# Second attention's projections in packed weight tiles

## The chip, the cores and the metric

The kernel runs on one core of one Trainium2 chip. The time is the device time of one execution in microseconds (us); the time before is a median of three runs. The profile shows one execution. Its engines are PE (TensorE, the matrix engine, with PEld for its weight loads), DVE (VectorE), ACT (ScalarE), POOL (GpSimd) and SP (SyncE, which issues the DMAs).

## The reference, cut to what matters

The program computes two transformer blocks on 512 tokens of width 1024. The second has a sparse attention (8 heads, called NSA here) and a second, latent attention (8 heads, MLA). Only the latter's projections change:

```python
def mla_attention(c_q, c_kv, k_rope, positions, q_norm_g, w_q_up, kv_norm_g, w_kv_up):
    q = (rms_norm_2(c_q, q_norm_g) @ w_q_up).reshape(B, S, H, MLA_NOPE_DIM + MLA_ROPE_DIM)
    q_nope = q[..., :MLA_NOPE_DIM]
    q_rot = rope(q[..., MLA_NOPE_DIM:], positions)
    kv = (rms_norm_2(c_kv, kv_norm_g) @ w_kv_up).reshape(B, S, H, MLA_NOPE_DIM + MLA_V_DIM)
    k_nope, v = kv[..., :MLA_NOPE_DIM], kv[..., MLA_NOPE_DIM:]
    k_rot = rope(k_rope[:, :, None, :], positions)[:, :, 0]
    scale = (MLA_NOPE_DIM + MLA_ROPE_DIM) ** -0.5
...
        s = (jnp.einsum('bqhd,bkhd->bhqk', qn, k_nope)
             + jnp.einsum('bqhd,bkd->bhqk', qr, k_rot)).astype(jnp.float32) * scale
        p = masked_softmax(s, key_idx[None, :] <= tc[:, None])
        return jnp.einsum('bhqk,bkhd->bqhd', p.astype(v.dtype), v)
```

A head's query has 64 plain and 32 rotated values; its key has 64 plain values of its own and the 32 rotated ones that all heads share. `w_q_up` is 256 x 768, `w_kv_up` 128 x 1024.

## The kernel before, in words

Each engine runs a program written out by hand. It waits on semaphores that count the steps of the others: `after(engine, who, name)` waits until `who` has done the step `name`, `done` marks a step, and the lists `STEPS` hold each engine's steps in order. Nothing is reordered while it runs.

The attention is a loop over 96 steps on every engine: steps 0 to 63 are NSA (query tiles of 128 by head and branch), 64 to 95 are MLA (eight heads `e` with four query tiles `qt` each, which see 128, 256, 384 and 512 keys). In step i TensorE runs

- `scores(i)`, queries as weights against the keys as moving data (L2854; the lines here are those of the profile);
- `fill(i, 4)`: four matmuls of the other work's stream, the input projections z0 to z7 up to step 63, nothing in steps 64 to 69, and the output projections oA, oB, oC from step 70 (`A_FIRST`), L2114;
- `jobs(i)`, odd work that belongs to certain steps;
- `turned(i - 2)` (L2863), two more matmuls of the stream, and `values(i - 3)` (L2877).

DVE takes the maximum of the scores (`most`) and adds the values up (`combine`), ACT does the exponential (`soft`) and copies the turned probabilities; each then has its own `jobs(i)`.

MLA's projections are such jobs. Head h has three: `q up h` in step 58 + 4h (two matmuls with 96 weight columns, L2689, one for each half of 256), `k up h` in the next step (one with 64 columns, L2695) and `rot up h` in the next (one with 96 rows and columns, which swaps the halves of the rotated part, L2701). ACT copies q up to `qraw` and k up to `km`; POOL multiplies `qraw` by the cosines (`rcos`, L1335), DVE the turned values by the sines (`rsin`, L2042) and adds the two to `qm` (L2047, step `q ready h`). The 64 plain rows pass through both with cosine 1 and sine 0. `qm` and `km` hold two heads. DVE copies the shared rotated keys to both halves of `km` once (L2034). `latent values c` (L2680, steps 63 to 66) makes the value rows of a token chunk.

The jobs write to two banks in turn: `aux_bank` gives a job one of them by its place in the table `JOBS`, and `job_free` waits for the reader of the job two places before.

At the change from NSA to MLA a chain begins. When the 64 NSA steps are added up, TensorE turns o_nsa (steps 67 and 68, L2706), DVE multiplies it by the gate (`mix`, step `mixed k`, L1925) into one of two buffers, ACT rounds it to `hhi` (`mix high k`, L1098), POOL takes the rest as `hlo` (`mix low k`, L1316) and frees the buffer. oA0 in step 70 waits for `mixed 3`, which frees its banks, and at each k for `mix low k`. A weight tile of the stream comes by SP's queue into one of four slots of `stage`, ACT rounds it to `whi` (L1001), POOL takes the rest as `wlo` (L1264).

Of the kernel before, what the change touches and what calls it, by code (L numbers as in the profile page):

```python
# [75 lines left out]
for _step in range(58, N_STEPS):  # L76
    if 63 <= _step < 67:
        JOBS[f"latent values {_step - 63}"] = ("act", f"latent values {_step - 63}")
    if _step < 58 + 4 * QH and _step % 4 == 2:
        JOBS[f"q up {(_step - 58) // 4}"] = ("act", f"ev q up {(_step - 58) // 4}")  # L80
    if 59 <= _step < 59 + 4 * QH and _step % 4 == 3:
        JOBS[f"k up {(_step - 59) // 4}"] = ("act", f"ev k up {(_step - 59) // 4}")
    if 60 <= _step < 60 + 4 * QH and _step % 4 == 0:
        JOBS[f"rot up {(_step - 60) // 4}"] = ("dve", f"sin up {(_step - 60) // 4}")
    if _step in (75, 83, 91):
        JOBS[f"turned {4 + (75, 83, 91).index(_step)}"] = ("dve", f"mixed {4 + (75, 83, 91).index(_step)}")
# [35 lines left out]
def shape_constants_2():  # L122
# [34 lines left out]
def build(nc, A, out, const_cols, const2_cols):  # L157
# [3 lines left out]
    with ctx:  # L161
# [187 lines left out]
        for name in """ident_in const_in nm_in nm_tr nm_col ones_set ba_hi eps_set x_sq x_rms x_inv x_dg xtr xev rs_ps x_f h_hi h_lo vec_in vec_tr vec_col out_done w_hi w_lo w_used n_sq n_acc  # L349
# [2595 lines left out]
```

## Time and profile before

| | us |
|---|---|
| median of 3 runs (1146.34 to 1147.6) | 1146.76 |
| the profiled execution | 1146.54 |
| its span in the profile | 1144.7 |
| PE busy | 1112.0 (97%) |
| DVE, ACT, POOL busy | 585.6, 469.9, 488.0 |
| PE waiting for another engine, from 940 on, all together | 5.0 |

The difference between the profiled execution and its span, 1.8 us, lies around the span. The profile counts an fp32 matmul of 512 columns as two records, so an "x2" in a timeline row is one matmul, and for L2689 an "x4" is one projection. A row's duration is that from its first start to its modelled last end, and overlaps the next row; what something costs TensorE is read from start to start.

### The profile page before, as it was taken

To read this page: it belongs to the slowest core of one execution; us is meant where nothing else is said; L and a number is where in the kernel's file an instruction comes from. 1 tells how busy PE (TensorE), PEld (TensorE's weight loads), DVE (VectorE), ACT (ScalarE), POOL (GpSimd) and SP (SyncE) were. 2 spreads that over 40 slices of the span, in tenths; PEclk is the share of its full clock that TensorE was granted. 3 is DMA by queue.
4 is the path that set the end of the run, shared out by engine and by line. 5 is a ranking of instruction groups with operands and counts; after the bars stand their busy time and mean duration, and the time that the engine had idled before them with its cause. 6 is when DMAs were issued, how large, how long until landed. Compare 5 with 4: busy or idle time off the path is not lost. (4 is left out here: it accounts for less than half of the span.)

```text
span 1144.7 us, 16590 instructions
## 1 busy us (share of the span) xinstructions
PE 1112.0 (97%) x5905; PEld 908.2 (79%) x5905; DVE 585.6 (51%) x1250; ACT 469.9 (41%) x1004; POOL 488.0 (43%) x281
## 2 busy tenths in 40 slices
PE   7999999999999999999999999999999999999996
PEld 6788888888878878878888888867888888556674
DVE  6687656665646556512112126446653664344466
ACT  6544346555543431431331233433333444343343
POOL 5776412232326775764574574453121211132220
PEclk9999999999999999999999999999999999999998
DMA  7544522211105354354354355332112100001011
GB/s 217 141 113 125 138 56 66 56 55 48 38 19 171 96 165 147 93 166 139 99 165 128 111 158 129 95 74 56 38 38 65 47 20 28 12 9 38 19 38 74
DMA packets 161046, 99.84 MB, mean 87 GB/s; under 512 B 24056, under 2 KB 154444, under 8 KB 159948
## 3 DMA queue, kind: packets, MB, share of 16 engines
q1 hardware_dynamic: 160812, 98.80, 29.8%
q8 instruction: 45, 0.74, 0.3%
q14 instruction: 29, 0.24, 0.1%
q10 hardware_dynamic: 160, 0.07, 0.0%
HBM read 95.69 MB, written 3.16 MB: 86 GB/s over the span
## 5 line engine op out<-in xcount | busy, mean ns | idle before, releaser
L1172 POOL TENSOR_TENSOR wlo<-stage,whi 128x1024 fp32r<-128x1024 f32 (+1 forms) x105 | 273.0, 2604 | 238.5 <-ACT whi L712 238.3
L2114 PE MATMUL ps<-hhi,whi 128*128 128x512 f32 (+1 forms) x728 | 297.8, 409 | 3.9 <-DVE gated L1925 2.2
L2114 PE MATMUL ps<-hhi,wlo 128*128 128x512 f32 (+1 forms) x728 | 293.9, 404 | 0.0
L2114 PE MATMUL ps<-hlo,whi 128*128 128x512 f32 (+1 forms) x728 | 285.0, 395 | 0.0
L2114 PEld LDWEIGHTS ps<-hhi,whi 128*128 128x128 f32 (+1 forms) x728 | 137.0, 188 | 44.4 <-issue 13.5
L712 ACT ACTIVATE whi<-stage 128x1024 fp32r<-128x1024 f32 x104 | 109.6, 1055 | 129.1 <-PE ps L2114 100.2
L1264 POOL TENSOR_TENSOR wlo<-stage,whi 128x1024 fp32r<-128x1024 f32 (+3 forms) x40 | 73.5, 1838 | 197.8 <-ACT whi L1001 197.8
L2114 PEld LDWEIGHTS ps<-hlo,whi 128*128 128x128 f32 (+1 forms) x728 | 137.0, 188 | 24.0
L2114 PEld LDWEIGHTS ps<-hhi,wlo 128*128 128x128 f32 (+1 forms) x728 | 137.4, 189 | 22.8 <-issue 2.8
L1078 ACT ACTIVATE prob<-ps,aneg 128x128 f32<-128x128 f32 (+1 forms) x96 | 50.7, 528 | 199.5 <-issue 102.2
L2114 PE MATMUL ps<-ahi,whi 128*128 128x512 f32 x320 | 127.8, 399 | 4.7 <-POOL alo L1252 3.0
L2114 PE MATMUL ps<-alo,whi 128*128 128x512 f32 x320 | 125.2, 391 | 0.0
L2114 PE MATMUL ps<-ahi,wlo 128*128 128x512 f32 x320 | 125.1, 391 | 0.0
L1683 DVE TENSOR_TENSOR hf<-relu 128x512 f32<-128x512 f32 x32 | 26.8, 837 | 113.3 <-ACT relu L977 109.7
L1689 DVE TENSOR_TENSOR xT<-xT,ps 128x512 f32<-128x512 f32 x32 | 22.0, 688 | 103.0 <-PE ps L2114 103.0
L2114 PEld LDWEIGHTS ps<-ahi,whi 128*128 128x128 f32 x320 | 60.2, 188 | 18.1 <-POOL alo L1252 4.7
L2114 PEld LDWEIGHTS ps<-alo,whi 128*128 128x128 f32 x320 | 60.1, 188 | 12.3
L2114 PEld LDWEIGHTS ps<-ahi,wlo 128*128 128x128 f32 x320 | 60.2, 188 | 11.1
L1981 DVE SCALAR_TENSOR_TENSOR o_nsa<-ps,acoef,o_nsa 128x64 f32<-128x64 f32 x64 | 18.1, 283 | 85.2 <-PE ps L2877 84.9
L1388 DVE SCALAR_TENSOR_TENSOR acc<-ps,convw,acc 128x511 f32<-128x511 f32 (+2 forms) x72 | 53.8, 747 | 11.6 <-ACT acc L745 9.9
L1951 DVE TENSOR_REDUCE amax<-ps 128x1 f32<-128x128 f32 (+1 forms) x96 | 46.8, 487 | 25.0 <-PE ps L2855 24.1
L977 ACT ACTIVATE relu<-ps 128x512 f32<-128x512 f32 x32 | 19.1, 598 | 93.8 <-PE ps L2114 93.8
(378 smaller groups left out, 1834.7 us busy)
## 6 DMA issues: line engine op xcount, KB each, us to landing
stage<-dn_w_in SPq DMA_DIRECT2D x32, 512.0 KB, 4.1
stage<-mlp_w_up SPq DMA_DIRECT2D x32, 512.0 KB, 4.6
stage<-mlp_w_down SPq DMA_DIRECT2D x32, 512.0 KB, 4.6
mod_w<-ada_w SPq DMA_DIRECT2D x8, 1536.0 KB, 6.3
stage<-w_in SPq DMA_DIRECT2D x17, 512.0 KB, 3.6
gcrow<-gc_rows SPq DMA_DIRECT2D x16, 256.0 KB, 3.3
stage<-dn_w_out SPq DMA_DIRECT2D x8, 512.0 KB, 3.6
stage<-w_in SPq DMA_DIRECT2D x9, 256.0 KB, 2.9
```

The lines of the kernel that those rows point to most:

```text
L712: act.activation(whi[:, slot, 0:ks, 0:cols], stage[:, slot, 0:ks, 0:cols], ACT.Copy).then_inc(s["w_hi"], 1)
L977: act.activation(relu[:, m % 2], up_bank(q, m), ACT.Relu).then_inc(s["mlp_relu"], 1)
L1078: act.activation(prob[:, i % 2, 0:keys], ps[:, 2 + i % 2, 0:keys], ACT.Exp, scale=SCALE if kind == "nsa" else SCALE_M, bias=aneg[:, i % 2: ...
L1172: pool.tensor_tensor(wlo[:, slot, 0:ks, 0:cols], stage[:, slot, 0:ks, 0:cols], whi[:, slot, 0:ks, 0:cols], ALU.subtract).then_inc(s["w_lo" ...
L1264: pool.tensor_tensor(wlo[:, n % RING, 0:ks, 0:cols], stage[:, n % RING, 0:ks, 0:cols], whi[:, n % RING, 0:ks, 0:cols], ALU.subtract).then_ ...
L1388: dve.scalar_tensor_tensor(out=a[:, t:T], in0=u[:, 0:T - t], scalar=convw[:, (3 - t) * 3 + seq, h:h + 1], in1=a[:, t:T], op0=ALU.mult, op1 ...
L1683: dve.tensor_tensor(af[:, m % 2], relu[:, m % 2], relu[:, m % 2], ALU.mult).then_inc(s["mlp_f"], 1)
L1689: dve.tensor_tensor(xT[:, m], xT[:, m], ps[:, (U_MLP + m) % 2, :], ALU.add).then_inc(s["res"], 1)
L1951: dve.tensor_reduce(amax[:, c], ps[:, 2 + i % 2, 0:(qt + 1) * P], AX.X, ALU.max).then_inc(s["at_max"], 1)
L1981: dve.scalar_tensor_tensor(out=o, in0=ps[:, 7, 0:DK], scalar=acoef[:, c], in1=o, op0=ALU.mult, op1=ALU.add)\
L2114: mm = pe.matmul(bank, w[:, slot, k - ks[0], 0:width], x[:, k], start=(i == 0), stop=(i == len(todo) - 1))
```

## The change

The 96-column tile of a head is taken apart. `wqr` holds the rotated parts of four heads side by side (4 x 32 = 128 columns, `q rope g`, g = 0 or 1), `wqn` the plain parts (two heads, 128 columns, `q up j`), `wkn` the plain keys (two heads, 128 columns, `k up j`). `rot up g` turns four heads at once. The plain parts go from the bank straight to their place: ACT copies each result in two halves of 64 rows, and cosine, sine and sum are made only on the rotated parts.

The scores then run over 128 rows rather than 96. A head's query tile holds its 64 plain rows and 64 rows with the rotated parts of itself and of another head. The key tile `km` has four slots: 64 plain rows, 32 rotated key rows against the head's own part (`rope_rows`), and 32 zero rows against the other's. POOL clears `km` in step 46 (`key rows`), and SP copies the rotated keys in by four DMAs in place of DVE's copies. `qm` is now `q2T`, whose NSA queries have been used by then.

The core of the diff (the step lists are left out; the table `JOBS` and the step numbers stand for them):

```diff
+JOBS.update({"q rope 0": ("act", "ev q rope 0"), "rot up 0": ("dve", "sin up 0"),
+             "q up 0": ("act", "ev q up 0"), "k up 0": ("act", "ev k up 0")})
+JOBS.update({f"latent values {_c}": ("act", f"latent values {_c}") for _c in range(CH)})
...
+ROPE_STEP, PAIR_STEP = (54, 71), (60, 66, 76, 84)
...
+        def rope_rows(h):
+
+            first = (1 - h % 2) * MN + h % 4 // 2 * MR
+            return slice(first, first + MR)
...
                 if name == "z5":
                     after(sp, "dve", "post q3")
-                    sp.dma_start(wq[:, :, :, :], A["w_q_up_2"][0].rearrange("(k p) (h c) -> p k h c", p=P, c=MD)).then_inc(s["wq_in"], 16)
+                    w_q = A["w_q_up_2"][0].rearrange("(k p) (h c) -> k p h c", p=P, c=MD)
+                    for k in range(2):
+                        for g, odd in itertools.product(range(2), range(2)):
+                            sp.dma_start(wqr[:, k, g, 2 - 2 * odd:4 - 2 * odd], w_q[k, :, 4 * g + odd:4 * g + 4:2, MN:])                                .then_inc(s["wq_in"], 16)
+                    for k in range(2):
+                        sp.dma_start(wqn[:, k], w_q[k, :, :, 0:MN]).then_inc(s["wq_in"], 16)
...
+                if name == "z7":
+                    after(sp, "pool", "key rows")
+                    after(sp, "dve", "post kr")
+                    for h in range(4):
+                        sp.dma_start(km[rope_rows(h), h], krT[MN:MD, :]).then_inc(s["kr_in"], 16)
...
+                if i in ROPE_STEP:
+                    g = ROPE_STEP.index(i)
+                    after(act, "pe", f"q rope {g}")
+                    if g:
+                        after(act, "dve", "z 7")
+                    done(act.activation(qraw[g][:, :], aux_bank(f"q rope {g}"), ACT.Copy), f"ev q rope {g}")
+                for j in range(QH // 2):
+                    for what, dst in enumerate((qm, km)):
+                        if i == PAIR_STEP[j] + what:
+                            name = f"{'qk'[what]} up {j}"
+                            after(act, "pe", name)
...
+                            for r in range(2):
+                                ins = act.activation(dst[group(r), 2 * j % 4 + r], aux_bank(name)[group(r)], ACT.Copy)
+                            done(ins, f"ev {name}")
...
+                if i in (57, 58, 59, 65, 77, 78, 79, 82):
+                    h = (57, 58, 59, 65, 77, 78, 79, 82).index(i)
+                    after(dve, "dve", f"sin up {h // 4}")
+                    after(dve, "pool", f"cos up {h // 4}")
+                    dve.wait_ge(s["at_s"], 16 * (h + 1) if h < 4 else N_NSA + 4 * (h - 3))
+                    r = group(1 - h % 2)
+                    done(dve.tensor_tensor(qm[r, h % 4], rcos[r, :], rsin[r, :], ALU.add), f"q ready {h}")
...
                     if qt == 0:
                         after(pe, "dve", f"q ready {e}")
-                        after(pe, "act", f"ev k up {e}")
-                    q, k = qm[0:MD, e % 2, qt * P:(qt + 1) * P], km[0:MD, e % 2, 0:(qt + 1) * P]
+                        after(pe, "act", f"ev k up {e // 2}")
+                        pe.wait_ge(s["kr_in"], 64)
+                    q, k = qm[:, e % 4, qt * P:(qt + 1) * P], km[:, e % 4, 0:(qt + 1) * P]
```

How the order changes, at three places. TensorE, from the job of step 66 to that of step 68, before (wkv,cn is `latent values 3`, cn,wq `q up 2`, cn,wkv `k up 2`, qraw `rot up 2`):

```order
L2680 MATMUL ps<-wkv,cn 128x512
L2689 MATMUL ps<-cn,wq 96x512 x2
L2863 MATMUL ps<-const,prob 128x128
L2877 MATMUL ps<-v_1_116,probT 128x64 x4
L2854 MATMUL ps<-km,qm 128x512
L2855 MATMUL ps<-negb,identb 128x128
L2695 MATMUL ps<-cn,wkv 64x512
L2706 MATMUL ps<-const,o_nsa 128x128 x8
...
L2855 MATMUL ps<-negb,identb 128x128
L2701 MATMUL ps<-qraw,const_121 96x512
L2706 MATMUL ps<-const,o_nsa 128x128 x8
```

The same place now (cn,wqn is `q up 1`, cn,wkn `k up 1`):

```order
L2697 MATMUL ps<-wkv,cn 128x512
L2720 MATMUL ps<-cn,wqn 128x512 x2
L2892 MATMUL ps<-const,prob 128x128
L2906 MATMUL ps<-v_1_116,probT 128x64 x4
L2883 MATMUL ps<-km,q2T 128x512
L2884 MATMUL ps<-negb,identb 128x128
L2728 MATMUL ps<-cn,wkn 128x512
L2733 MATMUL ps<-const,o_nsa 128x128 x8
...
L2884 MATMUL ps<-negb,identb 128x128
L2733 MATMUL ps<-const,o_nsa 128x128 x8
```

Step 66 keeps two projection matmuls, step 67 one, and step 68's is gone. Over the whole program 16 + 8 + 8 = 32 projection matmuls become 4 + 2 + 8 + 4 = 18: two in step 54, one in 55, two in 60, one in 61, two in 66, one in 67, two in 71, one in 72, two in 76, one in 77, two in 84, one in 85.

DVE, from `mixed 0` and `mixed 1` (step 67) to `mixed 2` and `mixed 3` (step 68), before:

```order
L1925 SCALAR_TENSOR_TENSOR gated<-ps,zs_139 128x512 x2
L1951 TENSOR_REDUCE amax<-ps 128x1
L1953 TENSOR_SCALAR aneg<-amax 128x1
L1959 RECIPROCAL ainv<-asum 128x1
L1985 TENSOR_SCALAR o_mla<-ps,ainv 128x64
L2042 TENSOR_TENSOR rsin<-ps,table 96x512
L2047 TENSOR_TENSOR qm<-rcos,rsin 96x512
L1925 SCALAR_TENSOR_TENSOR gated<-ps,zs_139 128x512 x2
```

The same place now:

```order
L1945 SCALAR_TENSOR_TENSOR gated<-ps,zs_139 128x512 x2
L1971 TENSOR_REDUCE amax<-ps 128x1
L1973 TENSOR_SCALAR aneg<-amax 128x1
L1979 RECIPROCAL ainv<-asum 128x1
L2005 TENSOR_SCALAR o_mla<-ps,ainv 128x64
L1945 SCALAR_TENSOR_TENSOR gated<-ps,zs_139 128x512 x2
```

The two operations of the rotation have gone from between the mixes.

SP's queue, from the loads of z5 on, before:

```order
L692 DMA wq<-w_q_up 128x2x768
L681 DMA stage<-w_in 128x8x128
L695 DMA wkv<-w_kv_up 128x1024
L681 DMA stage<-w_in 128x8x128
L674 DMA stage<-w_out 128x4x128 x8
L674 DMA stage<-w_out 128x2x128
L698 DMA grow<-final_norm_g 128x1024
L674 DMA stage<-w_out 128x2x128 x7
```

The same place now:

```order
L694 DMA wqr<-w_q_up 128x2x32 x8
L696 DMA wqn<-w_q_up 128x8x64 x2
L680 DMA stage<-w_in 128x8x128
L700 DMA wkn<-w_kv_up 128x8x64
L700 DMA wkv<-w_kv_up 128x8x64
L680 DMA stage<-w_in 128x8x128
L706 DMA km<-krT 32x512 x4
L673 DMA stage<-w_out 128x4x128 x8
L673 DMA stage<-w_out 128x2x128 x8
```

One load has become ten, one two, and four copies that wait for POOL's `key rows` stand ahead of all loads of w_out; `grow` goes behind the last of them.

## Rows read from the trace of the kernel before

**Rows 1.** Busy time by engine in four stretches; the last three columns: granted clock, DMA share, GB/s.

```profile
core 0: us, PE busy (x) PEld busy (x) DVE busy (x) ACT busy (x) POOL busy (x), PEclk, DMA share, GB/s
...
996.00:1019.00 23.00, 19.60 (x104) 12.14 (x103) 10.73 (x32) 11.07 (x29) 5.39 (x4) 1.00 0.04 11
1019.00:1040.00 21.00, 20.83 (x98) 13.90 (x99) 8.59 (x30) 9.18 (x25) 7.41 (x6) 1.00 0.11 38
...
1100.00:1108.00 8.00, 8.00 (x51) 6.73 (x50) 5.27 (x16) 4.41 (x11) 5.48 (x3) 1.00 0.01 3
...
1137.00:1145.00 8.00, 0.00 (x0) 0.00 (x0) 2.69 (x6) 1.73 (x2) 0.00 (x0) 0.50 0.64 262
```

**Rows 2.** Timeline of PE, scores alone: start, duration, names, weight tile, moving shape.

```profile
960.04 0.86 PE L2854 MATMUL ps<-kz,q2T 128*128 128x384 f32 x2
...
963.19 1.08 PE L2854 MATMUL ps<-kz,q2T 128*128 128x512 f32 x2
...
965.99 0.44 PE L2854 MATMUL ps<-kz,q2T 128*128 128x128 f32 x2
...
968.50 0.65 PE L2854 MATMUL ps<-kz,q2T 128*128 128x256 f32 x2
...
971.54 0.86 PE L2854 MATMUL ps<-kz,q2T 128*128 128x384 f32 x2
...
976.41 1.08 PE L2854 MATMUL ps<-kz,q2T 128*128 128x512 f32 x2
...
980.36 0.44 PE L2854 MATMUL ps<-kz,q2T 128*128 128x128 f32 x2
...
983.72 0.65 PE L2854 MATMUL ps<-kz,q2T 128*128 128x256 f32 x2
...
1000.21 0.65 PE L2854 MATMUL ps<-km,qm 96*128 96x256 f32 x2
```

**Rows 3.** PE's groups by line and shape, from 940 on: busy, mean ns of one.

```profile
L2689 PE MATMUL ps<-cn,wq 128*96 128x512 f32 x32 | 15.0, 592 | 0.0
```

**Rows 4.** Line 2579 alone, the rotation of NSA's queries: ns min/median/max.

```profile
L2579 PE MATMUL ps<-raw,const x12: 590/591/592, 757.0 to 850.3; 128*128 128x512 f32 x12
```

**Rows 5.** Timeline of PE, steps 64 to 71; in brackets the idle time before.

```profile
997.66 1.12 PE L2680 MATMUL ps<-wkv,cn 128*128 128x512 f32 x2 [0.71 <-ACT v_mla L1123]
...
1001.44 1.12 PE L2680 MATMUL ps<-wkv,cn 128*128 128x512 f32 x2 [0.53 <-ACT v_mla L1123]
...
1012.41 1.16 PE L2706 MATMUL ps<-const,o_nsa 128*128 128x128 f32 x8
...
1019.17 0.47 PE L2114 MATMUL ps<-hhi,whi 128*128 128x512 f32 x1 [2.20 <-DVE gated L1925]
...
1025.03 0.39 PE L2114 MATMUL ps<-hhi,whi 128*128 128x512 f32 x1
```

**Rows 6.** Timeline of DVE, steps 67 and 68.

```profile
1011.58 1.28 DVE L1925 SCALAR_TENSOR_TENSOR gated<-ps,zs 128x512 f32<-128x512 f32 x2
...
1015.24 0.69 DVE L2047 TENSOR_TENSOR qm<-rcos,rsin 96x512 f32<-96x512 f32 x1
1017.16 0.69 DVE L1925 SCALAR_TENSOR_TENSOR gated<-ps,zs 128x512 f32<-128x512 f32 x1 [1.23 <-POOL hlo L1316]
```

**Rows 7.** Timeline of POOL: the split of z6, and the low parts of the mix.

```profile
932.84 2.37 POOL L1264 TENSOR_TENSOR wlo<-stage,whi 128x1024 fp32r<-128x1024 f32 x1 [12.59 <-ACT whi L1001]
...
1015.42 1.63 POOL L1316 TENSOR_TENSOR hlo<-gated,hhi 128x512 fp32r<-128x512 f32 x1 [5.08 <-ACT hhi L1098]
...
1021.27 2.51 POOL L1316 TENSOR_TENSOR hlo<-gated,hhi 128x512 fp32r<-128x512 f32 x2 [3.00 <-ACT hhi L1098]
```

**Rows 8.** POOL's groups by line and shape, whole span: a memset of 2048 elements.

```profile
L1277 POOL MEMSET o_nsa<- 128x2048 f32 x1 | 1.8, 1805 | 0.0
```

**Rows 9.** Timeline of ACT: the first high part of w_out's weights.

```profile
955.53 0.64 ACT L1001 ACTIVATE whi<-stage 128x512 fp32r<-128x512 f32 x1
```

**Rows 10.** ACT's groups by line and shape, from 940 on.

```profile
L1136 ACT ACTIVATE km<-ps 64x512 f32<-64x512 f32 x8 | 4.7, 583 | 0.0
```

**Rows 11.** DMA issues by line: KB each, us to landing.

```profile
stage<-w_out SPq DMA_DIRECT2D x8, 256.0 KB, 2.6
```

More of the change, by code:

```diff
@@ L75 @@
         "block values 2": ("dve", "block out 2"), "block values 3": ("dve", "block out 3")}
[L76 to L86, printed above, removed]
+JOBS.update({"q rope 0": ("act", "ev q rope 0"), "rot up 0": ("dve", "sin up 0"),
+             "q up 0": ("act", "ev q up 0"), "k up 0": ("act", "ev k up 0")})
+JOBS.update({f"latent values {_c}": ("act", f"latent values {_c}") for _c in range(CH)})
+JOBS.update({"q up 1": ("act", "ev q up 1"), "k up 1": ("act", "ev k up 1"),
[3 rows of a table added]
+ROPE_STEP, PAIR_STEP = (54, 71), (60, 66, 76, 84)
 JOBS[f"turned {KT - 1}"] = ("dve", f"mixed {KT - 1}")
@@ L130, in shape_constants_2 @@
     parts["cmp_one"] = (seen * 1.0).reshape(P, -1)
-    for name, rows, first, width in (("rot", P, 0, 64), ("rot_m", P, 64, 32)):
+    for name, rows, first, width in (("rot", P, 0, 64), ("rot_m", P, 0, 32)):
         m = np.zeros((P, P))
@@ L139, in shape_constants_2 @@
     parts["swap"] = np.roll(np.eye(P), DK, axis=1)
-    for name, first, width in (("freq", 0, 64), ("freq_m", 64, 32)):
+    for name, first, width in (("freq", 0, 64), ("freq_m", 0, 32)):
         half = width // 2
@@ L404, in build @@
                 "kc rotated", "sin q3", "post q3", "scaled 0", "scaled 1", "max", "less max", "sum", "seen",
-                "sum inv", "coef", "probs", "z 0", "latent base q", "latent base", "cq 0", "cq 1", "rotated keys",
[6 rows of a table removed]
-                "sum oC1", "sum oC2", "sum oC3", "sum oC4", "sum oC5", "sum oC6", "sum oC7", "mixed 7", "mix low 7",
[3 rows of a table removed]
[10 rows of a table added]
             "pool": ["mlp low 1", "mlp low 3", "mlp low 5", "mlp low 7", "zero", "norm low 1", "norm low 3",
                 "norm low 5", "norm low 7", "cos ks", "cos q0", "cos kr", "cos kw", "inv 1", "window zero", "cos q1",
-                "cos q2", "block zero", "cos q3", "latent power", "cos up 0", "cos up 1", "cos up 2", "mix low 0",
-                "mix low 1", "mix low 2", "mix low 3", "cos up 3", "cos up 4", "mix low 4", "cos up 5", "cos up 6",
-                "mix low 5", "cos up 7", "mix low 6"],
+                "cos q2", "block zero", "cos q3", "latent power", "key rows", "cos up 0", "mix low 0", "mix low 1",
+                "mix low 2", "mix low 3", "cos up 1", "mix low 4", "mix low 5", "mix low 6"],
         }
@@ L1330, in _ @@
                     done(pool.tensor_tensor(lpow[:, :], lbase[:, :], minus_half[:, :], ALU.pow), "latent power")
-                if i >= 58 and (i - 58) % 4 == 0 and (i - 58) // 4 < QH:
-                    h = (i - 58) // 4
-                    after(pool, "act", f"ev q up {h}")
-                    after(pool, "dve", f"q ready {h - 1}" if h else "post q3")
-                    done(pool.tensor_tensor(rcos[0:MD, :], qraw[0:MD, h % 2], table[0:MD, 3], ALU.mult), f"cos up {h}")
+                if i == 46:
+                    after(pool, "pe", "block values 3")
+                    done(pool.memset(km[:, :, :], 0.0), "key rows")
+                if i in ROPE_STEP:
+                    g = ROPE_STEP.index(i)
+                    after(pool, "act", f"ev q rope {g}")
+                    after(pool, "dve", "q ready 3" if g else "post q3")
+                    done(pool.tensor_tensor(rcos[:, :], qraw[g][:, :], table[:, 3], ALU.mult), f"cos up {g}")
                 if i in (68, 69):
@@ L2031, in jobs @@
                                                   in1=aux_bank("latent root 1"), op0=ALU.mult, op1=ALU.mult), "ckv")
[L2032 to L2036 removed]
                 if i % 4 == 0 and 36 <= i <= 64:
                     z_silu(i // 4 - 9)
[L2039 to L2047 removed]
+                if i - 2 in ROPE_STEP:
+                    g = ROPE_STEP.index(i - 2)
+                    after(dve, "pe", f"rot up {g}")
+                    done(dve.tensor_tensor(rsin[:, :], aux_bank(f"rot up {g}"), table[:, 2], ALU.mult), f"sin up {g}")
+                if i in (57, 58, 59, 65, 77, 78, 79, 82):
[5 more added lines that the diff above has]
+                    done(dve.tensor_tensor(qm[r, h % 4], rcos[r, :], rsin[r, :], ALU.add), f"q ready {h}")
                 if i in (67, 68):
@@ L2677, in latent_values, with project_rope @@
                 job_free(pe, job)
-                pe.wait_ge(s["wv_in"], 16)
+                pe.wait_ge(s["wv_in"], 32)
                 after(pe, "dve", "ckv")
-                done(pe.matmul(aux_bank(job), cn[:, 2, c * P:(c + 1) * P], wkv[:, :, MN:], start=True, stop=True), job)
-            def project_q(h):
-                job = f"q up {h}"
+                done(pe.matmul(aux_bank(job), cn[:, 2, c * P:(c + 1) * P], wkv[:, :, :], start=True, stop=True), job)
+            def project_rope(g):
+                job = f"q rope {g}"
@@ L2690, in project_q, with project_rot @@
                 done(mm, job)
-            def project_k(h):
-                job = f"k up {h}"
+            def project_rot(g):
+                job = f"rot up {g}"
                 job_free(pe, job)
-                done(pe.matmul(aux_bank(job)[0:MN], wkv[:, h, 0:MN], cn[:, 2], start=True, stop=True), job)
-            def project_rot(h):
-                job = f"rot up {h}"
+                after(pe, "act", f"ev q rope {g}")
+                done(pe.matmul(aux_bank(job), K2["rot_m"], qraw[g][:, :], start=True, stop=True), job)
@@ L2699, in project_rot, with project_q, project_k @@
+            def project_q(j):
+                job = f"q up {j}"
                 job_free(pe, job)
-                after(pe, "act", f"ev q up {h}")
-                done(pe.matmul(aux_bank(job)[0:MD], K2["rot_m"][0:MD, 0:MD], qraw[0:MD, h % 2], start=True, stop=True), job)
+                for k in range(2):
+                    mm = pe.matmul(aux_bank(job), wqn[:, k, 2 * j:2 * j + 2].rearrange("p h c -> p (h c)"), cn[:, k], start=(k == 0), stop=(k == 1))
+                done(mm, job)
+            def project_k(j):
+                job = f"k up {j}"
+                job_free(pe, job)
+                pe.wait_ge(s["wv_in"], 32)
+                after(pe, "dve", "ckv")
+                done(pe.matmul(aux_bank(job), wkn[:, 2 * j:2 * j + 2].rearrange("p h c -> p (h c)"), cn[:, 2], start=True, stop=True), job)
@@ L2823, in jobs @@
                     latent_values(i - 63)
[L2824 to L2830 removed]
+                if i in ROPE_STEP:
+                    project_rope(ROPE_STEP.index(i))
+                if i - 1 in ROPE_STEP:
+                    project_rot(ROPE_STEP.index(i - 1))
+                if i in PAIR_STEP:
+                    project_q(PAIR_STEP.index(i))
+                if i - 1 in PAIR_STEP:
+                    project_k(PAIR_STEP.index(i - 1))
                 if i in (67, 68):
```

68 lines of the change are left out of this document (21 added, 47 removed), and 50 rows, old and new, of tables (JOBS, STEPS).

## The prediction

> **What bounds the kernel now.** I read the busy times of some stretches first. TensorE works through all 8.00 us of the stretch 1100 to 1108, and 20.83 of 21 us in the one from 1019 [rows 1]. Only the change from NSA to MLA differs: of the 23 us from 996 on, TensorE works 19.60. So a matmul taken out elsewhere shortens the span by its own cost. In the stretch with waits each removal has to be held against the chain that runs there. The waits stand in TensorE's timeline: 0.71 and 0.53 us for the copy of an earlier value chunk, 2.20 us for `mixed 3` [rows 5].
>
> **What a projection costs.** Its price is read from the start of one step's scores to the start of the next, against the same step four earlier, which has no projection.
>
> - `q up`: from 971.54 to 976.41 is 4.87 us, from 960.04 to 963.19 is 3.15. Difference 1.72 for two matmuls, 0.86 each [rows 2].
> - `k up`: from 976.41 to 980.36 is 3.95, from 963.19 to 965.99 is 2.80. Difference 1.15 for one matmul of only 64 columns [rows 2].
> - `rot up`: from 980.36 to 983.72 is 3.36, from 965.99 to 968.50 is 2.51. Difference 0.85 [rows 2].
>
> A head costs 3.72 us, the eight of them 29.8 us.
>
> The new matmuls have full tiles. A record of the 96-column projection lasts 592 ns [rows 3], one of a tile of 128 x 128 over the same 512 columns 591 ns [rows 4]. So the width costs nothing between 96 and 128, and I price each at 0.86 us; the 0.3 us more of the 64-column tile is gone too. 18 x 0.86 = 15.5 us. The least price is that 0.86; the most is the 1.15 of `k up`, which would add 18 x 0.29 = 5.2 us. I take the low end, since the 128 x 128 row is the same form.
>
> The scores over 128 rows cost no more than over 96: 256 keys take 0.65 us with NSA's full tile and 0.65 us with MLA's 96 rows [rows 2].
>
> On TensorE alone this gives 29.8 - 15.5 = 14.3 us.
>
> **The stretch of steps 64 to 70.** Here I go wait by wait.
>
> - `latent values 1` waited 0.71 us for the copy of chunk 0, and `latent values 2` 0.53 us for that of chunk 1 [rows 5], because `job_free` looks two places back in the table, and a `k up` or `rot up` stood between the chunks. Now chunk 1 looks back to `k up 0` of step 61, and chunk 2 to chunk 0, a step older. Both waits go: +1.2 us.
> - Step 68 loses `rot up 2` (0.85), after which TensorE turned o_nsa's third tile at 1012.41 [rows 5]. That needs `mixed 0`, the first of two operations begun at 1011.58 and lasting 1.28 together [rows 6]: done at about 1012.25. Of the 0.85 only 0.1 is won, so -0.75 us.
> - The wait of 2.20 us stays whole: it ends with `mixed 3`. Going back, `mixed 2` waited 1.23 us for POOL [rows 6], whose `mix low 0` began at 1015.42 and ended at 1017.05, 0.11 us before it [rows 6, 7]. No projection lies in this chain, but DVE's `qm` of head 2 does at its side: it ran from 1015.24 to 1015.93 [rows 6]. `mix low 0` took 1.63 us; the pair at 1021.27 took 2.51, so 1.26 each [rows 7]. With `q ready 2` gone from step 68 I take the excess back: +0.35 us.
> - Step 70 loses `q up 3` (1.72), and TensorE comes to the fourth k of oA0, at 1025.03 before, at 1023.31. That needs `mix low 3`, done at 1021.27 + 2.51 = 1023.78 [rows 5, 7]. A new wait: -0.5 us.
>
> By the Trainium skill (SBUF — State Buffer, section SBUF: two separate sides) a DVE operation with two SBUF inputs and a GpSimd one that reads SBUF lock each other out for the whole instruction. The row agrees in kind. By that rule `mix low 0` would lose the 0.51 us that `qm` still ran, and the sum would win 0.5 rather than 0.35; the row says 0.35 to 0.38.
>
> Together +0.3 us in this stretch. The sum is 14.3 + 0.3 = 14.6 us.
>
> **What lies beside TensorE.**
>
> - ACT copied 16 projection results of 0.58 us; a copy of 64 rows costs that much [rows 10], and the halves are now copied singly, so 2 + 16 = 18 copies, 1.2 us more over 30 steps. Two of them in one step take 1.2 us, queued ahead of the next exponential. ACT was busy 9.18 of 21 us [rows 1]; this hides behind the four stream matmuls that TensorE does before it needs the next probabilities. Uncovered, each of the eight pairs would cost 0.6.
> - DVE drops six `rsin` and two key copies; its eight `q ready` stay at about 0.69 [rows 6], one per step at most, and POOL drops six cosine products. Nobody waits for either.
> - POOL's memset of `km` has 2048 elements like that of o_nsa, 1.8 us [rows 8]. It comes behind the split of z6, which ends at 935.2 [rows 7], so it is done at about 937.
> - SP stands in its queue until then, with the four copies of the rotated keys and all loads of w_out behind it. A load of 256 KB lands in 2.6 us [rows 11]; ACT wants the first at 955.53 [rows 9]. Even with 5 us for the four issues it lands by 945. Slack 10 us, cost nothing. If the slack were used up, `whi` and with it ACT's whole row would be late.
> - The ten loads of w_q in small pieces go out where `wq` went and are needed in step 54, some 100 us on. Hidden.
> - `rot up` now follows its `q rope` after one step, not two. ACT's copy has to be done in between: about 2 us of exponential, probabilities and copy, against fill, values, scores and fill. It fits narrowly; bound 0 to 0.3 us each for two, I take 0.
>
> **The sum.** 1146.54 - 14.6 = 1131.9 for the profiled execution. The median lies 0.2 above it, so 1132.0 us, with a span near 1130.1. What a measurement of this kernel can tell from no change is about 0.2%, 2.3 us; the forecast is six times that.
>
> **The rivals.**
>
> - *The removed work comes back as waits (12%).* With fewer jobs a step lasts 2.5 to 3.15 us throughout, and the chain from scores by DVE's maximum and ACT's exponential to the turned probabilities could become the bound. From step 71 on TensorE gives up 9.2 us (four heads of 3.72 and the last two jobs of head 3, 16.9 together, less the nine matmuls of 0.86 that stand there now); half of it back is 1136.6, all of it 1141.2. Against it: in the stretch 1100 to 1108, steps without a projection and with a weight to split in each, TensorE does not wait at all [rows 1].
> - *More than forecast (5%).* Neither of the two new waits of 1.25 us appears, since ACT and POOL have less in steps 67 to 70: 1130.7; with a shorter chain to `mixed 3` too, 1129.
> - *The packed tile costs what it saves (2%).* If a full tile cost 1.65 us, 18 would cost the old 29.8, and the time would stay at 1146.8. Only [rows 4] speaks against it, but plainly.
> - *Slower (3%): the clock.* TensorE was granted 1.00 throughout the stretch with 3.4 us of idle time, the full 2.4 GHz, and 0.50, 1.2 GHz, in the last 8 us, in which it did nothing [rows 1]. The stretch now has as many waits but less work between them. Should the clock fall there, work of x us takes 2x; the gain is used up at x = 14.6, and the kernel is slower by a measurable amount from x = 16.9. With all the 20.83 us of work from 1019 to 1040 [rows 1] at half clock: 1132.0 + 20.8 = 1152.8. Against it, the waits add up to less than before: 1.2 us go and 1.25 come, in two pieces of 0.5 and 0.75, none longer than the 2.20 that was there at full clock.
>
> The Trainium skill (TensorE: Matmul & The Clock Gate, Part 1) states the same two levels and that idleness lowers the clock; the last stretch agrees.
>
> **How the numbers follow.** The forecast has 78%, with a range of its own from 1130.5 to 1133.5: the 0.3 us twice of `rot up`, the two new waits between nothing and double. The rest is the rivals'. From 1130.0 to 1135.5 lies the forecast, half of the first rival and half of the second: about 8 in 10 and a little more. Faster by over 0.2%: 78 + 12 + 5 = 95%. Within: 2%. Slower: 3%.
>
> **What the profile after would show.** Eighteen projection matmuls of records near 591 ns, none of 64 columns. `q up` in steps 76 and 84 costing 1.72, `k up` 0.86. No wait at `latent values`; one of about 0.7 us ahead of the turning of o_nsa's third tile, one of about 0.5 inside oA0; the one for `mixed 3` still near 2.2, `mix low 0` near 1.3. First w_out load at about 940, no wait for weights. Gapless TensorE from step 71 to 95. The prediction is wrong if waits for ACT or DVE stand between 1020 and 1095, if a full tile lasts longer than 0.86, or if the granted clock is below 1.00 there.

## The result and the profile after

The changed kernel takes 1132.49 us (median of 4 runs, 1131.1 to 1133.88) against 1146.78 us (4 runs, 1146.34 to 1147.6). The ratio is 0.9875, with a 95% interval from 0.9858 to 0.9892: 14.3 us less. Forecast were 1132.0 us and a range of 1130.0 to 1135.5. Eight more executions, in two later sets, gave medians of 1131.7 and 1131.95. The profiled execution took 1131.1 us over a span of 1129.3, 15.4 less than before in both. Of the span's 15.4, 0.5 was there before the first of the changed steps: the scores that began at 960.04 now begin at 959.51. That is chance: with the program the same up to there, they begin at 959.71 in e1 and at 960.57 in e10 below, both at full clock. The change itself gave 14.9.

The timeline of PE in the changed kernel, scores alone, over the steps in which the prices were read (the columns are those of [rows 2]; L2883 is what L2854 was):

```profile
959.51 0.86 PE L2883 MATMUL ps<-kz,q2T 128*128 128x384 f32 x2
...
964.37 1.08 PE L2883 MATMUL ps<-kz,q2T 128*128 128x512 f32 x2
...
979.54 0.44 PE L2883 MATMUL ps<-kz,q2T 128*128 128x128 f32 x2
...
983.75 0.65 PE L2883 MATMUL ps<-kz,q2T 128*128 128x256 f32 x2
...
987.65 0.86 PE L2883 MATMUL ps<-kz,q2T 128*128 128x384 f32 x2
```

The step with a packed `q rope` lasts 4.86 us, where the same step without a projection lasted 3.15 [rows 2]: 1.71 for two full tiles. A packed `q up` costs 4.21 less 2.51, 1.70; a packed `k up` 3.90 less 3.04, 0.86 [rows 2]. So a full tile costs 0.86, as forecast, and it carries two heads.

The timeline of PE from step 64 on, the rows in which a wait stood or was expected:

```profile
994.78 1.08 PE L2697 MATMUL ps<-wkv,cn 128*128 128x512 f32 x2
...
996.96 1.08 PE L2697 MATMUL ps<-wkv,cn 128*128 128x512 f32 x2
...
1007.64 1.16 PE L2733 MATMUL ps<-const,o_nsa 128*128 128x128 f32 x8 [0.73 <-DVE gated L1945]
...
1011.28 0.86 PE L2883 MATMUL ps<-km,q2T 128*128 128x384 f32 x2
1011.99 0.22 PE L2884 MATMUL ps<-negb,identb 128*128 128x128 bf16 x1
1014.03 0.47 PE L2131 MATMUL ps<-hhi,whi 128*128 128x512 f32 x1 [1.83 <-DVE gated L1945]
...
1014.81 0.39 PE L2131 MATMUL ps<-hhi,whi 128*128 128x512 f32 x1
1015.68 0.30 PE L2892 MATMUL ps<-const,prob 128*128 128x128 f32 x1 [0.48 <-ACT probT L1096]
...
1017.12 1.08 PE L2883 MATMUL ps<-km,q2T 128*128 128x512 f32 x2
...
1018.85 0.39 PE L2131 MATMUL ps<-hhi,whi 128*128 128x512 f32 x1
```

Against [rows 5]: both `latent values` run without a wait. A wait of 0.73 us stands ahead of the turning of o_nsa's third tile. The one for `mixed 3` is 1.83 instead of 2.20. Behind it stands a new one of 0.48 us, ahead of the turning of probabilities in step 70. The fourth k of oA0, at 1018.85, does not wait.

Behind step 72, from 1030 to 1090, TensorE has no gap. Windows of the changed kernel (columns as in [rows 1]):

```profile
994.00:1013.00 19.00, 17.34 (x100) 11.89 (x99) 8.03 (x27) 11.67 (x30) 3.62 (x3) 1.00 0.05 14
1013.00:1030.00 17.00, 15.48 (x78) 11.10 (x79) 7.41 (x26) 7.28 (x20) 6.24 (x6) 1.00 0.03 9
1030.00:1090.00 60.00, 60.00 (x333) 46.38 (x333) 31.21 (x95) 29.48 (x80) 15.38 (x15) 1.00 0.13 43
```

POOL's two low parts behind the wait for `mixed 3`, in its timeline:

```profile
1010.65 2.48 POOL L1333 TENSOR_TENSOR hlo<-gated,hhi 128x512 fp32r<-128x512 f32 x2 [12.68 <-ACT hhi L1108]
1016.13 2.50 POOL L1333 TENSOR_TENSOR hlo<-gated,hhi 128x512 fp32r<-128x512 f32 x2 [2.99 <-ACT hhi L1108]
```

`mix low 0` and `1` are one row now, 1.24 each; the first had been 1.63 [rows 7].

### The profile page after: what moved, and what is told of

Same layout as the page of the kernel before. It is cut to its first block and busy times, and to the rows that moved or that the text cites. A ratio compares the mean times of both kernels' runs of the same rounds, so it can differ in the third digit from the quotient of the medians.

```text
span 1129.3 us, 16534 instructions
## 1 busy us (share of the span) xinstructions
PE 1097.3 (97%) x5877; PEld 906.1 (80%) x5877; DVE 580.0 (51%) x1242; ACT 471.8 (42%) x1006; POOL 481.4 (43%) x276
```

## The experiments

Each kernel was run beside the kernel before, on the same chip; the three medians of the latter are 1147.23, 1147.14 and 1146.85 us. The mean granted clock of an execution is given where it matters. It is 0.997 in an execution in which it falls only at the end, where TensorE has nothing left to do.

**e1 and e12, the changed kernel again.** No edit.

> The changed kernel once more, for its spread. Its four executions so far were two near 1131.3 us at a granted clock of 0.997 and two near 1133.6 at 0.994. Theory one (the clock): TensorE's granted clock is lower for a while in some executions, because of the waits around steps 68 to 70, so that two groups about 2.3 us apart come again, each with its clock. Theory two (chance): the executions fill the range from 1131 to 1134 evenly, and the clock says nothing of the time. The median is 1131 to 1134 in both.

> The changed kernel beside e11, on the same chip, to see how often its clock falls. Clock theory: about one execution in three at 0.994 and near 1133.7, the others at 0.997 and 1131.1 to 1132.1. Rival (that was chance): executions spread evenly. Median 1131.3 to 1133 in both.

e1: 1131.7 us (4 executions), ratio 0.987 [0.9855, 0.9885]. e12: 1131.95 us, 0.9865 [0.9843, 0.9886]. With the first four that is twelve: seven at a clock of 0.997, from 1131.09 to 1132.11 us, one at 0.995 and 1132.46, four at 0.994, from 1133.12 to 1133.88. The clock does sort the times. Where it falls in the changed kernel no profile shows, since all three fell on executions at 0.997; e5, e9 and e11 show it for kernels near to it.

**e2, the kernel before with wide `k up`.**

```diff
-                done(pe.matmul(aux_bank(job)[0:MN], wkv[:, h, 0:MN], cn[:, 2], start=True, stop=True), job)
+                done(pe.matmul(aux_bank(job), wkv[:, h, :], cn[:, 2], start=True, stop=True), job)
```

> The kernel before, with each of the eight `k up` projections computed over 128 weight columns instead of 64; the reader takes the first 64 rows as it did, so no result changes. Theory (the 64-column tile is what makes `k up` cost 1.15 us where a matmul of 96 costs 0.85): 8 x 0.29 = 2.3 us less than the kernel before, about 1144.4 us, `k up` costing 0.86. Rival (the width doesn't matter, the 0.3 us is a matter of its place in the step): no change, 1146.8 us.

Timeline of PE, and behind it line 2695 alone (ns min/median/max of one):

```profile
976.82 1.08 PE L2854 MATMUL ps<-kz,q2T 128*128 128x512 f32 x2
...
980.48 0.44 PE L2854 MATMUL ps<-kz,q2T 128*128 128x128 f32 x2
```

```profile
L2695 PE MATMUL ps<-cn,wkv x16: 590/591/647, 978.8 to 1085.9; 128*128 128x512 f32 x16
```

The step takes 3.66 us instead of 3.95 [rows 2], so a `k up` of twice the width costs 0.86, and the span of the profiled execution is 1.8 us shorter although its step began 0.41 late (976.82 for 976.41). In the profile the theory holds to 0.1 us. The median does not show it: 1146.9 us, ratio 0.9996 [0.9987, 1.0005]. Only the profiled execution, 1144.66 us, had a clock of 0.997; the other ten had 0.993 to 0.996. Like beside like, the gain is in the times too: its three executions at 0.995 took 1145.22 to 1146.96 us, the seven of the kernel before at 0.995 beside it 1147.17 to 1147.83.

**e3 and e5, the packed key projection cut into 64-column matmuls again.** e3 is the first diff, e5 changes one line of it.

```diff
-                done(pe.matmul(aux_bank(job), wkn[:, 2 * j:2 * j + 2].rearrange("p h c -> p (h c)"), cn[:, 2], start=True, stop=True), job)
+                for r in range(2):
+                    mm = pe.matmul(aux_bank(job)[group(r)], wkn[:, 2 * j + r], cn[:, 2], start=True, stop=True)
+                done(mm, job)
```

```diff
-                for r in range(2):
+                for r in (0, 0, 1):
```

> The changed kernel with each of the four packed key projections as two matmuls of 64 columns into the two halves of the bank. Theory (a 64-column matmul costs 1.15 us, a full one 0.86): 4 x (2 x 1.15 - 0.86) = 5.8 us more, about 1138 us. Rival (only the number of matmuls counts): 4 x 0.86 = 3.4 us more, about 1135.8 us.

> The kernel of e3 with the first of its two 64-column matmuls issued twice in each of the four key projections (the repeat writes the same values, so no result changes). In e3 the second 64-column matmul cost 0.02 us, and its records lie side by side with the first's. Theory (two tiles go at once only because they stand in different halves of the columns): the repeat stands behind its twin in the same half and costs at least 0.43 us, at most 0.86 each; 4 of them are 1.7 to 3.4 us over e3, about 1134.9 to 1136.6. Rival (a 64-column matmul behind another is nearly free wherever it goes): as e3, 1133.2 us.

e3 took 1133.17 us, ratio 0.988 [0.9865, 0.9895]: 1.5 over e1 instead of 5.8 or 3.4, so both theories were wrong. The step with a `k up`, in e3 and then in e5:

```profile
984.51 0.65 PE L2885 MATMUL ps<-kz,q2T 128*128 128x256 f32 x2
...
986.14 1.08 PE L2729 MATMUL ps<-cn,wkn 128*64 128x512 f32 x4
...
988.72 0.86 PE L2885 MATMUL ps<-kz,q2T 128*128 128x384 f32 x2
```

```profile
985.60 0.65 PE L2885 MATMUL ps<-kz,q2T 128*128 128x256 f32 x2
...
987.23 1.93 PE L2729 MATMUL ps<-cn,wkn 128*64 128x512 f32 x6
...
990.66 0.54 PE L2885 MATMUL ps<-kz,q2T 128*128 128x384 f32 x1
```

A matmul leaves two records. In e3 the four of one pair, each near 0.6 us long, together take 1.08, no more than the two of a single one before. The step is 4.21 us, 0.31 over the changed kernel's 3.90. So the pair costs 1.17 us, against 1.15 for a single `k up` before, and the second 64-column matmul 0.02. In e5 the repeat into the same half makes it 5.06 us, 0.85 more. e5 as a whole took 1138.73 us, at clocks from 0.993 to 0.996; its execution at 0.996 took 1136.87, where e3's 1133.17 and 4 x 0.85 make 1136.57. Two 64-column tiles in different halves of the array go side by side, and what a 64-column matmul costs over a full one is paid once for the pair.

The Trainium skill (TensorEngine Tiling (Array Packing), section Tiling Modes) says both: that different tiles can load and multiply in parallel, and that a change of the tiling mode drains the engine. The runs agree with the first, by 0.02 against 0.85 us. The second fits the 0.3 us that stand once per pair between full tiles, and not once per matmul; that these 0.3 are the drain, no run shows by itself.

**e4 and e7, work put into the waits.** e4 moves `q rope 1` (from step 71; the expectation names 75) to step 70 ahead of the stream, e7 also `k up 1` from step 67 to 68.

```diff
-                if i in ROPE_STEP:
-                    project_rope(ROPE_STEP.index(i))
+                if i == ROPE_STEP[0]:
+                    project_rope(0)
...
+                    if i == A_FIRST:
+                        project_rope(1)
```

```diff
-                if i - 1 in PAIR_STEP:
-                    project_k(PAIR_STEP.index(i - 1))
+                if i in (61, 68, 77, 85):
+                    project_k((61, 68, 77, 85).index(i))
```

> The changed kernel with the second rotated projection, two full matmuls, put in step 70 between the scores and the stream, where TensorE waits 1.83 us for `mixed 3`, instead of in step 75. Theory (that wait hangs on DVE's and POOL's chain alone and takes in other work): 1.7 us less, about 1130.8 us at the clock of 1.00, with a wait of about 0.1 us left. Rival (the chain moves along with the work, or the wait comes back later in oA0): no change, about 1132.5 us.

> The kernel of e4 with the second packed key projection also moved: from step 67 to step 68, in front of the turning of o_nsa's third tile, where TensorE waits 0.73 us for `mixed 0`; ACT copies its result out in step 70. Theory (that wait, too, hangs on DVE's first product alone): 0.7 us less than e4, about 1129.9 us, the wait of 0.73 gone. Rival (TensorE gets to the second tile's turning earlier, so that DVE starts earlier and the wait only moves along): less still, as much as 0.86. Second rival (the copy on ACT, now among the `mix high` steps, delays the rounding of o_nsa or step 69's exponential): no gain or a loss of up to 1.2 us, with the wait for ACT's probabilities grown from 0.48.

PE in e4, from the scores of step 70, and then in e7 from the turning of o_nsa on:

```profile
1013.09 0.86 PE L2883 MATMUL ps<-km,q2T 128*128 128x384 f32 x2
...
1013.84 1.94 PE L2707 MATMUL ps<-cn,wqr 128*128 128x512 f32 x4
1015.85 0.47 PE L2131 MATMUL ps<-hhi,whi 128*128 128x512 f32 x1
```

```profile
1006.08 1.04 PE L2733 MATMUL ps<-const,o_nsa 128*128 128x128 f32 x8
...
1007.68 1.08 PE L2728 MATMUL ps<-cn,wkn 128*128 128x512 f32 x2
1008.59 1.15 PE L2733 MATMUL ps<-const,o_nsa 128*128 128x128 f32 x8
...
1014.98 0.47 PE L2131 MATMUL ps<-hhi,whi 128*128 128x512 f32 x1
```

In e4 the stream begins 2.76 us after the scores, as in the changed kernel (2.75), with 1.72 us of work in between: the chain to `mixed 3` did not move. From the scores of step 67 to those of step 72 it is 16.68 us instead of 18.37. e4 took 1130.58 us, ratio 0.9852 [0.9837, 0.9867], though all its executions have clocks of 0.995 or 0.996. In e7 the wait of 0.73 is gone and the stream begins 0.87 earlier than in e4. The first rival there was right: the turning of the second tile comes 0.87 earlier, so DVE does too. ACT's wait is 0.48 as before. e7 took 1130.25 us (5 executions, 1127.94 to 1130.52), ratio 0.9844 [0.9829, 0.9859]. Its median is the lowest, 1.6 us under the changed kernel's of twelve, but its interval overlaps those of e4 and e1: that e7 is faster than they is read from the timelines, not from the times.

**e6 and e11, the wait in step 70 filled with nothing useful, and lengthened.** e6 issues 14 matmuls that nobody reads ahead of the stream of step 70; e11 adds two reductions that nobody reads ahead of `mixed 3`.

```diff
+                    if i == A_FIRST:
+                        job_free(pe, "q rope 1")
+                        keep_busy(5 + list(JOBS).index("q rope 1") % 2, 14)
```

```diff
+                for x in range(2 if k == 3 else 0):
+                    dve.tensor_reduce(junk[:, x:x + 1], zs2[:, 2], AX.X, ALU.add)
                 done(dve.scalar_tensor_tensor(out=gated[:, k % 2], in0=bank, scalar=0.5, in1=zs2[:, k],
```

> The changed kernel with 14 matmuls of 128 columns that nobody reads ahead of the stream in step 70, in the 1.83 us that TensorE waits there for `mixed 3`. No work is saved. Clock theory (the executions at a clock of 0.994, some 2.3 us longer, lose it behind this wait): they vanish, all executions lie within 1131.0 to 1132.2 and the clock is 0.997. Rival (they lose it elsewhere; in the profile of e4 the clock fell to 0.50 near 734 us, between the two blocks): one execution in three still lies near 1133.7 at 0.994. In both the profile shows the wait filled and the span otherwise as it was.

> The changed kernel with two reductions of 128 x 512 elements, 0.69 us each and read by nobody, on DVE ahead of `mixed 3`, so that TensorE's wait in step 70 grows from 1.83 to about 3.2 us. Plain theory (a wait costs its own length): 1.4 us more than the changed kernel, 1132.7 at a clock of 0.997. Clock theory (behind this wait TensorE's clock can fall to 0.50, as the profile of e5 showed at 1020 us for 1.6 us; a longer wait makes it happen in more executions): most executions have a clock of at most 0.995 and lie at 1134.3 or above, and the profile shows granted clock below 1.00 between 1015 and 1025 us.

e6 took 1132.84 us (1132.27 to 1133.38), ratio 0.9872 [0.9856, 0.9887]. The filling took 3.1 us where some 2 were free, so the stream began 1.1 late. No execution is below 0.995, but the times did not keep to the range that I gave. e11 took 1134.34 us (1132.8 to 1136.22), ratio 0.9883 [0.9863, 0.9902], with clocks of 0.993, 0.994, 0.994, 0.996 and 0.996: no execution is at 0.997. Of the clock theory, three of five are at most 0.995, as expected, but one of these took only 1134.21, and one at 0.996 took 1134.34. The place is seen in the windows of two kernels, first e5, whose wait of 1.84 us ended at 1018.15, then e11, whose wait of 3.02 us ended at 1017.42:

```profile
1018.00:1020.00 2.00, 1.35 (x6) 0.91 (x7) 1.47 (x8) 1.40 (x4) 0.00 (x0) 0.97 0.00 0
1020.00:1022.00 2.00, 2.00 (x9) 1.81 (x9) 0.00 (x0) 1.42 (x5) 1.75 (x2) 0.50 0.00 0
1022.00:1024.00 2.00, 2.00 (x8) 1.20 (x8) 0.28 (x1) 0.00 (x0) 0.76 (x1) 0.68 0.00 0
```

```profile
1016.00:1018.00 2.00, 0.58 (x2) 0.52 (x3) 1.97 (x7) 0.13 (x1) 0.00 (x0) 0.76 0.00 0
1018.00:1020.00 2.00, 2.00 (x7) 1.47 (x6) 0.78 (x4) 2.00 (x6) 0.48 (x1) 0.50 0.00 0
1020.00:1022.00 2.00, 2.00 (x12) 1.47 (x11) 0.28 (x1) 0.69 (x3) 2.00 (x2) 0.89 0.00 0
```

The granted clock goes from 1.00, the full 2.4 GHz, to 0.50, 1.2 GHz, and comes back after about 3 us. In e5 the stretch from the stream's first matmul in step 70 to its first in step 71 lasts 5.66 us (1018.15 to 1023.81) instead of 4.03: 1.6 us lost. The same stretch lost 1.0 us in e9 (1015.54 to 1020.60) and 0.7 in e11 (1017.42 to 1022.16).

It also falls at two places that the change doesn't touch. Windows of e4, ahead of the second block, where TensorE issues small matmuls without a gap, and of e7, in the first block, behind a gap at 42 to 44 us:

```profile
732.00:734.00 2.00, 2.00 (x17) 2.00 (x16) 0.86 (x5) 1.02 (x2) 1.20 (x1) 0.76 0.00 0
734.00:736.00 2.00, 2.00 (x11) 2.00 (x11) 0.00 (x0) 0.00 (x0) 2.00 (x2) 0.50 0.09 14
```

```profile
42.00:44.00 2.00, 1.16 (x10) 0.93 (x8) 0.26 (x1) 0.99 (x2) 2.00 (x4) 1.00 0.02 5
...
46.00:48.00 2.00, 2.00 (x7) 1.59 (x6) 1.90 (x5) 0.87 (x2) 2.00 (x1) 0.59 1.06 324
48.00:50.00 2.00, 2.00 (x6) 1.55 (x5) 1.97 (x7) 0.91 (x2) 2.00 (x4) 0.55 0.46 86
```

The profiles at 0.995 (e4, e6, e7) have one fall, those at 0.993 and 0.994 (e5, e9, e11) two: one near 734 us and one behind the wait in step 70. With the wait standing, the second never came without the first, nor the first without the second (three profiles with both; the kernel before, the changed one, e1, e2, e3, e8, e10 and e12 with neither). What ties them no run shows.

Counted over all executions, those at 0.994 or less are 7 of 22 with the wait of 1.83 us as it is (the changed kernel, e3, e5, e8, e10), 4 of 6 with a longer one (e9, e11), and none of 13 with the wait filled (e4, e6, e7). So the wait in step 70 is a place where kernels with it can lose their clock, e5 with the changed kernel's own 1.8 us. For the changed kernel's four executions near 1133.6 us it is inferred, since none of them was profiled, and by the three profiles with two falls a part of their 2 us is lost near 734 us. The length of the wait is not all: the kernel before, with 2.20 us, is at 0.993 in 3 of 33 executions, and e2, with the same wait, at 0.994 or less in 6 of 11.

**e8, e9 and e10, what slowed `mix low 0`.** e8 moves `q ready 3` on DVE from step 65 to 68, between `mixed 1` and `mixed 2`; e9 adds a wait to it; e10 leaves it in step 65 and puts a reduction there that nobody reads. The first diff is e9's, and e8's without its last two lines; the second is e10's.

```diff
-                if i in (57, 58, 59, 65, 77, 78, 79, 82):
-                    h = (57, 58, 59, 65, 77, 78, 79, 82).index(i)
+                if i in (57, 58, 59, 68, 77, 78, 79, 82):
+                    h = (57, 58, 59, 68, 77, 78, 79, 82).index(i)
...
+                    if h == 3:
+                        after(dve, "act", "mix high 0")
```

```diff
+                if k == 2:
+                    after(dve, "act", "mix high 0")
+                    dve.tensor_reduce(junk[0:64, 0:1], zs2[0:64, 0], AX.X, ALU.add)
```

> The changed kernel with DVE's `q ready 3`, a sum of two tensors of 64 x 512, in step 68 between `mixed 1` and `mixed 2`, where the kernel before had one, instead of in step 65. Theory (it slows POOL's `mix low 0` beside it, the step that `mixed 2` waits for): `mix low 0` goes from 1.24 back to about 1.6 us and `mixed 3` ends about 0.37 us later, the wait in step 70 goes from 1.83 to about 2.2. Rival (the long `mix low 0` of before had another cause): `mix low 0` stays at 1.24, the wait at 1.83.

> The kernel of e8, in which `q ready 3` had ended 0.2 us before `mix low 0` began; here it also waits for `mix high 0`, for which `mix low 0` waits too, so that both begin together, as before the change. Theory (the sum on DVE slows POOL's difference beside it): the pair `mix low 0` and `1`, 2.48 us in the changed kernel, takes about 2.85, and TensorE's wait in step 70 grows from 1.83 to about 2.2. If one shuts the other out for as long as it lasts, 0.68 us: 3.16 and 2.5. Rival (no connection): 2.48 and 1.83.

> The changed kernel with one operation added on DVE beside `mix low 0`: a sum over 64 x 512 elements of one SBUF tensor into a scratch column that nobody reads, as long as the 64 x 512 sum of two tensors in e9 but with one input. Theory (only a DVE operation with two SBUF inputs slows POOL): the pair `mix low` stays at 2.48 and the wait in step 70 at 1.83. Rival (any DVE operation on SBUF does): as e9.

e8, e9 and e10 have one execution each. In e8 (1131.49 us) nothing changed, but the sum on DVE ran from 1010.13 to 1010.81 and POOL began at 1011.02: they did not meet, and the run decides nothing. In e9 (1133.62 us, clock 0.994) they do. POOL (its two differences singly behind it, as ns min/median/max) and DVE in e9, then in e10:

```profile
1011.71 2.94 POOL L1333 TENSOR_TENSOR hlo<-gated,hhi 128x512 fp32r<-128x512 f32 x2 [12.68 <-ACT hhi L1108]
...
L1333 POOL TENSOR_TENSOR hlo<-gated,hhi x2: 1265/1486/1706, 1011.7 to 1012.9; 128x512 fp32r<-128x512 f32 x2
...
1011.76 1.75 DVE L2066 TENSOR_TENSOR q2T<-rcos,rsin 64x512 f32<-64x512 f32 x1 [0.86 <-ACT hhi L1108]
1013.45 0.67 DVE L1945 SCALAR_TENSOR_TENSOR gated<-ps,zs 128x512 f32<-128x512 f32 x1
```

```profile
1011.72 2.49 POOL L1334 TENSOR_TENSOR hlo<-gated,hhi 128x512 fp32r<-128x512 f32 x2 [12.68 <-ACT hhi L1109]
...
1011.74 0.68 DVE L1946 TENSOR_REDUCE junk<-zs 64x1 f32<-64x512 f32 x1 [0.83 <-ACT hhi L1109]
1013.02 0.69 DVE L1949 SCALAR_TENSOR_TENSOR gated<-ps,zs 128x512 f32<-128x512 f32 x1 [0.60 <-POOL hlo L1334]
```

In e9 POOL's pair takes 2.94 instead of 2.48, and the sum on DVE, which began 0.05 us after POOL, 1.75 instead of 0.68. TensorE's wait in step 70 is 2.28. So the two do hinder each other, by the size expected, but not the step expected: `mix low 0`, which had begun first, kept its 1.27, DVE's sum waited behind it, and the 0.45 fell on `mix low 1` (1.71), which met the sum as it ran. `mixed 3` needs `mix low 1`, so its time is set by the pair. In e10 both keep their times (2.49 and 0.68), the wait stays at 1.83, and the execution took 1132.14 us, 1.0 over the changed kernel's profiled one; that was there before (the scores at 959.51 begin at 960.57).

e10 has one SBUF input in place of two, but it also writes only one column, so it alone doesn't tell input from output. The changed kernel does, where `mixed 2` runs beside `mix low 1`, the second of the pair from 1010.65 to 1013.13:

```profile
1012.02 0.69 DVE L1945 SCALAR_TENSOR_TENSOR gated<-ps,zs 128x512 f32<-128x512 f32 x1 [2.17 <-POOL hlo L1333]
1013.24 0.69 DVE L1945 SCALAR_TENSOR_TENSOR gated<-ps,zs 128x512 f32<-128x512 f32 x1 [0.53 <-POOL hlo L1333]
```

It reads one tensor in SBUF (`zs`; the other input is a bank) and writes 128 x 512 elements, and takes 0.69 beside POOL as `mixed 3` does almost clear of it. So it is the second SBUF input that matters.

The Trainium skill (SBUF — State Buffer, section SBUF: two separate sides) says that of such a pair the one that starts first shuts the other out for its whole length. e9 agrees: by that rule DVE waits out the 1.2 us that POOL's first 1.27 still ran, and it lost 1.07. In the kernel before, DVE was first and POOL lost 0.39 [rows 6, 7], where the rule gives 0.51.

## Why the prediction was right

**The price of a projection** held to 0.02 us in every step. The rival of a full tile at 1.65 us is refuted, by the 1.71 for two and by e2, and the removed work did not come back as waits: 60.00 of 60 us are busy from 1030 to 1090. From step 72 on the forecast's own prices give 9.7 us; found are 9.8. But my sentence that the width costs nothing between 96 and 128, and that a narrower tile costs more, was half of it. The 0.29 us of `k up` is the price of a 64-column tile among full ones, not of 64 columns (e3, e5). Two such tiles into the two halves win all but 0.3 us of a packed pair of `k up` (e3); for `q up` that was not tried.

**The waits at `latent values`** were mis-sized: +1.2 us in the sum. Steps 64 and 65 got 1.79 and 0.74 us shorter; less the 0.85 of a `rot up` that is 1.68. The bracket in [rows 5] counts from the modelled end of the matmul before (0.22 us), but an undisturbed successor starts 0.05 us after its start. So 0.71 in brackets are 0.88 from start to start, and 0.53 are 0.70; 0.1 of the 1.68 stays unexplained.

**Step 68**: forecast 0.1 us won of 0.85; the step lasts 2.95 us in both kernels, so nothing. The wait of 0.73 us is the forecast one. `mixed 0` began at 1006.82 and, at the 0.69 us of `mixed 2`, was done at 1007.51; TensorE began 0.13 later, a delay that the forecast left out. The same sum for the kernel before gives 1012.40, and TensorE began there at 1012.41: `rot up 2` had only just filled the wait.

**`mixed 3`**: forecast 0.35 us from the freed `mix low 0`; the wait fell by 0.37. e9 shows a POOL difference lengthened by 0.45 by DVE's sum, e10 none lengthened by a reduction. The rest of the wait depends on DVE and POOL alone (e4).

**The new wait of 0.5 us in step 70** came in that size, but the step that I named for it failed. It stands at the turning of probabilities, not at the fourth k of oA0. `mix low 3` was done at 1018.63, and TensorE came to that matmul at 1018.85. I had followed one consequence of `mixed 3` and not the other: DVE takes the next maximum only behind it, ACT stands 3.39 us for that maximum, and TensorE needs the bank that ACT copies out afterwards. `q up 3` had covered this. In start-to-start time it is 0.64 us.

**What was put at nothing** stayed at nothing. POOL cleared `km` from 934.61 to 936.42, SP issued the first load of w_out at 939.00, and ACT used it at 955.00; neither `rot up` waited.

**The clock.** The rival of 1152.8 us supposed that 20.8 us of work go at half clock. A fall at the place that the rival named is real in e5, e9 and e11, for about 3 us, at 0.7 to 1.6 us. I had argued that the waits add up to less than before. That did not protect the kernel: it is below 0.995 in 4 of 12 executions, the kernel before in 3 of 33. At 0.995 or 0.996 it is the other way round, 1 of 12 against 16 of 33. So it does not lose its clock more often than the kernel before; only the larger losses come more often, and with such counts that may still be chance.

**The time.** 1132.0 us was forecast as median, by way of 1131.9 for a profiled execution at full clock; that one took 1131.1. Of the 0.8 us between them 0.5 is the earlier start and 0.3 the waits. That the median came within 0.5 us is partly luck: two of its four executions (four of all twelve) lose 2 us of clock, which no term of the sum held, and the seven at 0.997 lie up to 0.9 us below the forecast or just above it.

Not tried: a kernel with the falls near 45 and 734 us removed, and a profile of the changed kernel in an execution at 0.994. Open is why e2 falls so often.

## What to carry to other kernels

Read the price of a matmul from the start of a step to the start of the next, against the same step without it; a bracket of idle time after a matmul misses the part that would have been overlapped. When work that covered a wait is removed, follow every consumer of the late step, not only the one that was seen waiting. A wait that hangs on a chain of other engines is a free place for TensorE's own work: 2.6 us of projections put there cost nothing (e4, e7), and the clock did not fall behind that place.

## What the runs showed of the hardware that was not expected

- Two 128 x 64 weight tiles in different halves of the columns cost 1.17 us together; a third, in the same half as the first, cost 0.85 more (e3, e5).
- A sum of two SBUF tensors on DVE took 1.75 instead of 0.68 us when it began 0.05 us behind a POOL subtraction, and the next subtraction took 1.71 instead of 1.26 (e9); a reduction of one tensor in its place took 0.68 (e10).
- TensorE's granted clock fell from 1.00 to 0.50 for about 3 us also where it issued small matmuls without a gap, near 734 us, in four of twelve experiments' profiles (e4, e5, e9, e11). It cost e4 1.56 us there: the small matmuls from 732.68 to the stream's next at 738.55 took 5.87 us, the same ones in the changed kernel 4.31.
